# A two-block transformer kernel on one core: normalised memory made earlier and kept, its first key projection run between the mLSTM head products

## What is computed

```python
memn = rmsnorm(mem, mem_norm)
for l in range(DEPTH):
    h = rmsnorm(x, mix_norm[l])
    x = x + (ab_mixer(...) if l % 2 == 0 else c_mixer(...))
    x = x + mem_cross_attn(rmsnorm(x, xa_norm[l]), memn, xa_wq[l], xa_wk[l], xa_wv[l], xa_wo[l])
    x = x + sq_relu_mlp(rmsnorm(x, mlp_norm[l]), mlp_w1[l], mlp_w2[l])
```

## Time and profile before

| | us |
|---|---|
| median of 3 runs | 1683.62 |
| lowest, highest run | 1671.38, 1685.43 |
| the profiled execution, its own time | 1661.19 |
| its span in the profile | 1659.4 |
| PE busy | 1573.6 (95% of the span) |
| POOL busy | 1188.4 (72%) |
| ACT busy | 827.7 (50%) |
| DVE busy | 768.3 (46%) |

### The profile page before, as it was taken

The page is one execution under the profiler, slowest core; times in us unless marked ns, Lnnn a source line. Parts: engine busy times, 40 slices in busy tenths (PEclk is TensorE's granted clock), DMA queues, the critical chain, the costliest instruction groups (busy, mean ns, idle before and its releaser), DMA issues.

```text
span 1659.4 us, 32836 instructions
## 1 busy us (share of the span) xinstructions
PE 1573.6 (95%) x12756; PEld 1496.2 (90%) x12756; DVE 768.3 (46%) x1402; ACT 827.7 (50%) x1242; POOL 1188.4 (72%) x920
## 2 busy tenths in 40 slices
PE   7989999999999898999999999989999999999997
PEld 5978989999988787998999998959999997899996
DVE  5547245220077666554422015865554227465523
ACT  4664445654456433544565455455545443554542
POOL 5654975999967600398589996805999997189994
PEclk9998999999999999999999999989999999899999
DMA  7432533555544300254355553404555654155552
GB/s 266 146 102 92 184 131 128 194 196 194 190 153 154 114 1 1 77 178 153 115 191 193 196 195 132 149 26 147 197 191 192 195 185 140 38 179 191 192 195 97
DMA packets 67231, 248.56 MB, mean 150 GB/s; under 512 B 7584, under 2 KB 7840, under 8 KB 66592
## 3 DMA queue, kind: packets, MB, share of 16 engines
q1 hardware_dynamic: 67104, 246.69, 44.5%
HBM read 245.62 MB, written 1.05 MB: 149 GB/s over the span
## 4 chain that ended last, share of the span: by engine, by line
PE 48%; POOL 22%; issue 21%; DVE 6%; ACT 2%; POOLq 0%; DVEq 0%; ACTq 0%
PE ps_dve L370 43%; POOL ring_lo L336 22%; PE ps_act L370 4%; DVE x_lo L1424 1%; PE ps_act L381 1%; DVE xT L1406 1%; DVE work L1474 1%; ACT x_hi L984 0%; ACT work L1029 0%; DVE work L1892 0%; DVE xT L1442 0%; ACT work L974 0%; DVE work L1889 0%; DVE sq L1435 0%; DVE work L1878 0%
## 5 line engine op out<-in xcount | busy, mean ns | idle before, releaser
L336 POOL TENSOR_TENSOR ring_lo<-ring,ring_hi 128x512 fp32r<-128x512 f32 x916 | 1188.2, 1332 | 449.7 <-ACT ring_hi L960 447.2
L960 ACT ACTIVATE ring_hi<-ring 128x1024 fp32r<-128x1024 f32 x458 | 466.0, 1052 | 207.7 <-DMA ring<-panels 198.2
L370 PE MATMUL ps_dve<-x_hi,ring_hi 128*128 128x256 f32 x1928 | 461.1, 280 | 26.8 <-DVE x_lo L1424 15.4
L370 PE MATMUL ps_dve<-x_lo,ring_hi 128*128 128x256 f32 x1928 | 456.8, 278 | 0.0
L370 PEld LDWEIGHTS ps_dve<-x_hi,ring_hi 128*128 128x128 f32 x1928 | 364.7, 189 | 32.6 <-DVE x_lo L1424 17.2
L370 PEld LDWEIGHTS ps_dve<-x_lo,ring_hi 128*128 128x128 f32 x1928 | 364.9, 189 | 0.5 <-issue 0.2
L370 PE MATMUL ps_dve<-x_hi,ring_lo 128*128 128x256 f32 x1928 | 270.4, 277 | 0.1
L370 PEld LDWEIGHTS ps_dve<-x_hi,ring_lo 128*128 128x128 f32 x1928 | 243.2, 189 | 0.3 <-POOL ring_lo L336 0.3
L370 PE MATMUL ps_dve<-work_parts,ring_hi 128*128 128x256 f32 x1728 | 225.3, 276 | 0.0
L370 PEld LDWEIGHTS ps_dve<-work_parts,ring_hi 128*128 128x128 f32 x1728 | 211.8, 188 | 0.0
L1442 DVE TENSOR_TENSOR xT<-xT,ps_dve 128x512 f32<-128x512 f32 x40 | 27.5, 688 | 323.9 <-PE ps_dve L370 323.7
(11 more groups left out here) (272 smaller groups left out, 2022.4 us busy)
## 6 DMA issues: line engine op xcount, KB each, us to landing
ring<-panels SPq DMA_DIRECT2D x458, 512.0 KB, 3.3
consts<-constants SPq DMA_DIRECT2D x1, 2208.0 KB, 12.6
xT<-x_t SPq DMA_DIRECT2D x1, 1024.0 KB, 5.2
memn<-mem_t SPq DMA_DIRECT2D x1, 1024.0 KB, 18.8
out_t<-xT SPq DMA_DIRECT2D x1, 1024.0 KB, 3.9
smalls<-small_operands SPq DMA_DIRECT2D x1, 808.5 KB, 15.7
consts<-constants SPq DMA_DIRECT2D x1, 129.5 KB, 5.0
angle_i<-positions SPq DMA_DIRECT2D x1, 128.0 KB, 7.7
```

The source lines that it names most:

```text
L336: pool.tensor_tensor(ring_lo[:, s, cs], ring[:, s, cs], plain(ring_hi[:, s, cs]), ALU.subtract).then_inc(sem("lo_made"), 1)
L370: ins = pe.matmul(o, lhsT, rhs, start=start, stop=stop, skip_group_check=True)
L960: tell(act.activation(ring_hi[:, n % RING, :], ring[:, n % RING, :], ACT.Copy), "hi_made")
```

## The change

It has three parts.

- The memory lands in `scratch`; DVE normalises it there in stick-breaking rounds 2 and 3, and makes high and low parts in rounds 3 and 4, into two tensors of their own, `mem_hi` (over the old `memn`) and `mem_lo` (new). Both layers read these; the second layer's `mem_parts` goes.
- On PE each of the four pairs of `xk0` panels runs in one mLSTM step, behind the step's products; after the heads comes the first pair of `xv0` panels, then the two head-norm products, then the other three pairs. ACT copies the key banks out between its `ml_w` steps, and takes the head norms after the first value bank, without loading its function table again.
- To make room for `mem_lo`, the constant `sel` shrinks from 1,024 columns to 8 and is spread where it is used (DVE writes `sel` into the work area, 4 x 128 columns, after `gate_scans`; ACT makes the two other copies from the spread form), and the integer positions share their place with `cosT`.

```diff
-                    ("sel", 8 * P), ("pick", 8 * 8)):
+                    ("sel", 8), ("pick", 8 * 8)):
...
-        memn = sb("memn", [P, C, T])
+        memn, mem_hi = sb_over("memn", "mem_hi", [P, C, T], F32, F32R)
+        mem_lo = sb("mem_lo", [P, C, T], F32R)
...
-        cosT = sb("cosT", [P, T])
+        angle_i, cosT = sb_over("angle_i", "cosT", [P, T], I32, F32)
...
+        sel = area(WORK - ML_H * P, ML_H, P)
+        sel_wide = const("sel").rearrange("p (h c) -> p h c", c=1).broadcast_to((P, 8, P))
...
-            sp.dma_start(memn[:, :, :], mem_in).then_inc(sem("memory_here"), 16)
+            sp.dma_start(scratch[:, :, :], mem_in).then_inc(sem("memory_here"), 16)
...
-            def memory_side(after=None):
-                project("act", "mem_keys", x_parts, C, 8, need=pairs_of("mem_parts"), after=after)
-                project_tokens("act", "mem_values", x_parts, 4)
+            mem_parts = (mem_hi, mem_lo)
+
+            def memory_keys(tiles, after=None):
+                project("act", "mem_keys", mem_parts, C, tiles, after=after)
+
+            def memory_values(banks):
+                project_tokens("act", "mem_values", mem_parts, banks)
...
+            told.more("sel_wide")
             ml_rows(0)
             for s in range(ML_H + 1):
...
                 if s:
                     ml_out(s - 1)
-            def mlstm_norms(i):
-                for g in range(2 if i == 1 else 0):
-                    told.more("squared")
-                    mm(bank("act", "norm_used"), ones, sq[:, 2 * g:2 * g + 2, :], True, True, "act")
-            memory_side(mlstm_norms)
+                if s == 0:
+                    told.more("mem_parts", C // 2)
+                if s < ML_H:
+                    memory_keys(2)
+            memory_values(1)
+            for g in range(2):
+                told.more("squared")
+                mm(bank("act", "norm_used"), ones, sq[:, 2 * g:2 * g + 2, :], True, True, "act")
+            memory_values(3)
...
-            memory_side(first_half_sums)
+            memory_keys(8, first_half_sums)
+            memory_values(4)
...
-            for h in range(ML_H):
-                told.more("ml_d")
...
-            reach("xk0", 0)
+            told.more("memory_normed", C)
+            for h in range(ML_H + 1):
+                if h < ML_H:
+                    told.more("ml_d")
+                    for j in range(2):
+                        ins = act.activation(ml_w[h % 2][:, j, :], ml_d[h % 2][:, j, :], ACT.Exp,
+                                             bias=ab_cols[:, 4 * j + h:4 * j + h + 1])
+                    tell(ins, "ml_w")
+                if h:
+                    memory_keys(0, h - 1)
             for g in range(2):
                 told.more("ml_h", 2)
                 tell(act.activation(sq[:, 2 * g:2 * g + 2, :], hm[:, 2 * g:2 * g + 2, :], ACT.Square), "squared")
-            memory_side(0, 0, 2)
-            rsqrt(2 * T, 1.0 / P)
-            told.more("memory_normed", C)
-            rsqrt(2 * T, 1.0 / P)
-            memory_side(0, 2, 4)
+            memory_values(0, 0)
+            rsqrt(2 * T, 1.0 / P, loaded=True)
+            rsqrt(2 * T, 1.0 / P, loaded=True)
+            for p in range(1, 4):
+                memory_values(0, p)
...
             scaled(ml_q, take())
+            tell(dve.tensor_copy(sel, sel_wide[:, 0:ML_H, :]), "sel_wide")
...
+                if s in (2, 3):
+                    renorm(scratch, small("mem_norm"), "memory_normed", memory_f, slice(4 * s - 8, 4 * s - 4))
+                if s >= 3:
+                    for c in range(4 * s - 12, 4 * s - 8, 2):
+                        in_parts(mem_hi, mem_lo, scratch, slice(c, c + 2), "mem_parts")
                 if s == 0:
                     scaled(ml_k, take(), 64 ** -0.5)
...
-            renorm(memn, small("mem_norm"), "memory_normed", memory_f)
...
-                    in_parts(x_hi, x_lo, memn, slice(2 * s, 2 * s + 2), "mem_parts")
...
-            mem_parts()
             told.more("gate_silu")
```

## The result

The changed kernel takes 1693.68 us (median of 8 runs, 1687.87 to 1698.19); the kernel before 1678.27 us (8 runs, 1663.99 to 1685.43). The ratio is 1.0108, with an interval of 1.0076 to 1.0140. The forecast was 1676 us in a range of 1660 to 1687, so it missed in sign and size; it gave 5% to a time over 1% slower. Three chips were used, so the ratios can be held against each other, and the medians only roughly.

A forecast was written before the change was run, and what follows sets the result against it. TensorE ends the work, so what counts is its waits and clock. Gain 11.2 - 2.2 - 1.7 = 7.3 us, taken from the median 1683.6, gives 1676 us, range 1660 to 1687.

The forecast's parts named there:

- Edits at nothing, or nearly: Second layer's dropped memory parts, constants shrunk by 1,016 columns, and the `sel` spread: each charged 0 us.
- the clock staying at half: Rival for the interleaved heads: light products keep TensorE's clock at half, 28 us slower after the 11.2; 3%.
- DVE held by POOL: Rival in stick-breaking rounds 3 and 4: normalisations cost 1.5 us each, pairs 3.1; kernel 2.9 us slower; 7%.
- The interleaving (+11.2): Heads with key panels between: TensorE neither waits nor slows, output projection starts at 177.3 instead of 188.5, gain 11.2 us.
- The wait for DVE (2.2): Last stick-breaking rounds: DVE's normalisations and pairs delay ACT's last exponential to 114.1; TensorE, ready at 111.90, waits 2.2 us.
- The clock (1.7): After that wait, dense key products run at a lowered clock for a while: 1.7 us lost, charged once.
- The cover too thin: DVE's head-norm chain before the output projection: done at +18.2, TensorE arrives at +19.0; charged 0.
- the third rival: DVE's chain to the output projection ends 2 to 3 us late, clock dips again: gain 2 to 4 us; 12%.
- The second layer: 0: Second layer loses four pairs of parts, 4.7 us of DVE, covered by TensorE's own delta rule work: 0 gained.
- the forecast gain of 7.3 us: Whole kernel: 11.2 gained, less a 2.2 us wait and 1.7 us of lowered clock.

The follow-up runs named there:

- the front pad: The kernel before with 32 unused bytes ahead of `ring_hi`, so weights and moving tensors all lie 32 bytes higher: 1670.73 us, ratio 0.9984.

## Why the prediction was wrong, point by point

**The failed step is "Edits at nothing, or nearly", where the constants that shrink by 1,016 columns are charged with 0.** I priced the shorter transfer, which is indeed worth nothing: TensorE's last wait at the start ends at 16.37 now, as in the earlier trace rows. I didn't price what a smaller tensor does to the addresses of all that is allocated behind it. This edit cost 44.0 us by the sum over the products, against the one fast profile of before; against the profiles with 224 and 480 bytes of pad the same sum gives 36 and 30. In whole kernels, 32 bytes of padding that bring the same distance cost the old one 1.51%, 25 us, and 224 bytes that take it away turn the changed one from a ratio of 1.0108 into 0.9922, some 31 us. The gain for which the change was made, some 10 us in its stretch, is outweighed two and a half to four times. None of my rivals held this mechanism. Of the two on the slower side, the clock staying at half did not occur, and DVE held by POOL occurred only in part: the pairs were held, the normalisations were not, since they ended at 105.20 and POOL began at 105.30, a margin of 0.1 us that I had not worked out.

**The interleaving (+11.2) was right in kind and somewhat small.** At equal distance the whole change gives 10.6 us, in the two profiles 9.9, after the losses below. I had expected 7.3 after them. With the 0.9 and 1.7 below the 9.9 make 12.5. The 11.2 also hid two causes in one number: undoing the interleaving alone gave back 6.9, and the parts made early have the rest.

**The wait for DVE (2.2) was oversized: 0.93.** The rows after, DVE and then PE (start, duration, what, [idle before <- releaser]):

```profile
103.53 1.67 DVE L1421 SCALAR_TENSOR_TENSOR scratch<-scratch,smalls,rstd 128x256 f32<-128x256 f32 x4
105.23 0.43 DVE L1427 CAST mem_hi<-scratch 128x512 fp32r<-128x512 f32 x1
105.70 1.64 DVE L1428 TENSOR_TENSOR mem_lo<-scratch,mem_hi 128x512 fp32r<-128x512 f32 x1
107.38 1.39 DVE L1427 CAST mem_hi<-scratch 128x512 fp32r<-128x512 f32 x1
108.80 1.67 DVE L1428 TENSOR_TENSOR mem_lo<-scratch,mem_hi 128x512 fp32r<-128x512 f32 x1
110.51 0.69 DVE L1602 SCALAR_TENSOR_TENSOR work<-ps_dve,stream_f 128x512 f32<-128x512 f32 x1
...
111.96 0.69 DVE L1666 TENSOR_TENSOR work<-work,consts 128x512 f32<-128x512 f32 x1
```

```profile
113.37 1.13 PE L371 MATMUL ps_act<-work 128*128 128x256 f32 x4 [0.93 <-ACT work L1151]
114.43 0.28 PE L382 MATMUL ps_dve<-consts,work 4*128 4x4 f32 x2
114.57 3.02 PE L371 MATMUL ps_dve<-work 4*128 4x512 f32 x8
117.52 0.39 PE L371 MATMUL ps_act<-mem_hi,ring_hi 128*128 128x256 f32 x1
```

The four normalisations took 1.67 us where I had taken 2.65, half of a group of eight in which one had been held. The two pairs took 5.24 (105.23 to 110.47), against my 5.3: POOL held three of four. The last head's two instructions ran free. So DVE was done at 112.65 and not at 113.5, ACT's exponential followed 0.8 us sooner than forecast, and TensorE itself arrived 0.5 us later, at 112.44 instead of 111.90. DVE was held while POOL worked from 105.30 on (6.33 us for four halves, 5.0 to 5.1 when alone), and that slowed POOL too.

**The clock (1.7) was right in this profile, and no constant.** After the stop, key products run 0.21 us apart from 118.20 to 120.76 and then 0.12 apart; 3.4 us at half clock are 1.7 lost. It did not stay at half. Of the nine profiles with the new order, six have 3.4 us at half clock here, two 6.8 and one 10.2, a loss of 1.7 to 5.1 us. This is the one with 480 bytes of pad, to be held against the 126 products at 0.97 above; its output projection began at 182.3:

```profile
120.00:140.00 20.00, 20.00 (x117) 17.05 (x116) 5.91 (x9) 7.69 (x13) 10.75 (x9) 0.85 0.23 79
```

**The cover too thin: a wait, where I had charged 0.** DVE's chain began with the first factor at 162.81 and ended at 180.9. TensorE began the output projection at 178.7 and stopped for the last part:

```profile
179.21 1.65 DVE L1428 TENSOR_TENSOR mix_lo<-mixT,mix_hi 128x512 fp32r<-128x512 f32 x1
```

```profile
180.92 0.39 PE L371 MATMUL ps_dve<-mix_hi,ring_hi 128*128 128x256 f32 x1 [1.32 <-DVE mix_lo L1428]
```

So the third rival occurred in small, with 1.3 us of wait. The chain from the first factor took 18.1 us instead of 16.0. The pairs at the end took 3.1 each in both kernels. The difference lies at the chain's start, which now falls into POOL's work (28.56 us from 159.70): its two gain instructions took 1.97 us and the gating 1.67, where before, with POOL starting only at 158.17, they took 0.88 and 0.69.

**The second layer: 0, and not tested by itself.** The keys begin at 686.29 instead of 682.89, after the delta rule's products (677.02, for which the profile shows the same wait of 0.85 us as before). That it is 3.4 us later, in spite of the gain, goes by the slower intervals since 180; I haven't summed them to that place.

**The number.** At the old distance the changed kernel ran at 0.9922 and 0.9907, a gain of 13 and 16 us with intervals from 7 to 19 and from 10 to 22. So the forecast gain of 7.3 us was at or below the low end for the change without its displacement. The mix of the two rates in a run moves this by several us.

## What to carry to other kernels

An edit that changes the size of an on-chip tensor moves all that is allocated behind it: count that as a part of the change, and before judging the change, pad the tensor back to its old size, or where the room is needed, as here, to the same place modulo 256 bytes. When a kernel gets slower with all engines as busy, and with waits and clock as before, count the products per window in a stretch that the edit did not touch; 178 against 171 in 20 us told of the loss here, and no wait, chain or busy share showed it. Where TensorE is the bound, the distance of the moving tensor from the weights is a parameter to tune, worth up to 6% on each product here.

## What was not expected of the hardware

The start-to-start time of a product of 128x128 weights with 256 moving columns, in dense stretches at full clock, took 113.3 to 120.0 ns by the distance of its two operands in a partition, on a period that is neither 32 nor 128 bytes; a step of 256 left the rates as they were. The Trainium skill (SBUF — State Buffer, section "SBUF: two separate sides") says that on the engine side only the port pair shared by GpSimd and DVE causes contention, and that PE never waits on anyone. That is a rule on waits between engines, and the products without any other engine or DMA beside them, 113.3 and 118.3 ns, show a slowing that needs no other engine. TensorE's weight load and its moving reads overlap in time, and how fast they go depends on where both lie. That they collide in the memory is my reading; the runs show the distance, not the place of a collision.

At distance 192 two rates exist, 113.3 and 117.8 ns. The kernel before had 117.8 in the input projection, in the memory products of both layers and around 220 to 240 us, and 113.3 elsewhere. The rate doesn't belong to the place: with 32 bytes of pad ahead of the ring the input projection ran at 113.5 until 60 us, and the products from 1160 to 1340 at 117.8. The two rates fit the wide runs at this distance (21.4 us over 8 runs of the kernel before, 25.5 over 10 with the front pad, 29.7 over 12 with 224 bytes) against 10 to 18 us over the 8 to 10 runs of each kernel at another distance; the runs' own rates weren't read, only those of the profiles. What selects the rate when a stretch begins is open; so are distances from 96 to 160, which weren't run.
